# The rotary turn of the second block's queries and key: products on TensorE, or transfers inside SBUF with a signed sine table

## The reference, cut to what matters

```python
half = HEAD_DIM // 2                                  # 32
ang = positions[..., None] * inv_freq                 # inv_freq has 32 values
cos, sin = jnp.cos(ang), jnp.sin(ang)
t1, t2 = tf[..., :half], tf[..., half:]
out = jnp.concatenate([t1 * cos - t2 * sin, t2 * cos + t1 * sin], axis=-1)
...
q = _rope(q.reshape(b, s, N_Q_HEADS, HEAD_DIM), positions)   # 8 heads of 64
k = _rope(k.reshape(b, s, N_KV_HEADS, HEAD_DIM), positions)  # 2 heads of 64
```

## Time and profile before

| what | value |
|---|---|
| device time, median of 3 runs (lowest to highest) | 1407.65 us (1406.44 to 1407.67) |
| span of the profiled execution (first to last instruction) | 1405.4 us, 20877 instructions |
| what the median has beyond that span | 2.25 us |
| busy: PE, DVE, ACT, POOL | 1387.1, 811.0, 478.8, 128.2 us |
| mean granted TensorE clock | 0.999 of full speed |

### The profile page before, as it was taken

How to read it: one execution, slowest core, us unless ns; L and a number is a source line. 1 busy time by engine, 2 the same in 40 slices (tenths; PEclk the granted TensorE clock), 3 DMA queues, 4 the chain that set the end, 5 groups by cost and what they waited for, 6 DMA issues and landing times.

```text
span 1405.4 us, 20877 instructions
## 1 busy us (share of the span) xinstructions
PE 1387.1 (99%) x8982; PEld 1106.9 (79%) x8982; DVE 811.0 (58%) x1142; ACT 478.8 (34%) x723; POOL 128.2 (9%) x134
## 2 busy tenths in 40 slices
PE   7999999999999999999999999999999999999998
PEld 5687887878778888887778888887887877888886
DVE  7375654646558745354575664546635435776654
ACT  6332324234145343234431221223333233444323
POOL 1020302002002011001210000000040012000000
PEclk9999999999999999999999999999999999999999
DMA  5111211111042333322255542332222333211362
GB/s 189 60 46 32 76 32 62 46 46 61 32 166 93 102 126 114 106 75 76 90 180 190 198 166 93 102 97 90 90 90 75 98 97 105 90 61 61 97 172 90
DMA packets 42204, 136.15 MB, mean 97 GB/s; under 512 B 4649, under 2 KB 8361, under 8 KB 42112
## 3 DMA queue, kind: packets, MB, share of 16 engines
q1 hardware_dynamic: 33984, 114.57, 25.3%
q0 software_dynamic: 4080, 14.65, 2.7%
q10 hardware_dynamic: 4048, 5.59, 1.2%
HBM read 130.34 MB, written 2.10 MB: 94 GB/s over the span
## 4 chain that ended last, share of the span: by engine, by line
PE 94%; DVE 3%; DMA 1%; ACT 1%; issue 0%; ACTq 0%; DVEq 0%
PE bank L418 92%; PE bank L421 2%; DVE w_lo L1424 1%; DVE opA_lo L1432 1%; DMA xT<-x 1%; DMA w_raw<-panels 0%; DVE tmp L1432 0%; ACT scores L934 0%; DVE P L1432 0%; ACT w_hi L934 0%; DVE scores L1424 0%; ACT opA_hi L934 0%; DVE sine L1432 0%; DVE cosine L1432 0%; DVE angle L1428 0%
## 5 line engine op out<-in xcount | busy, mean ns | idle before, releaser
L1424 DVE TENSOR_TENSOR w_lo<-w_raw,w_hi 128x1024 fp32r<-128x1024 f32 (+1 forms) x209 | 256.6, 1228 | 358.9 <-ACT w_hi L934 358.6
L418 PE MATMUL bank<-opA_hi,w_hi 128*128 128x512 f32 x1000 | 410.7, 411 | 11.0 <-DVE opA_lo L1432 8.6
L418 PE MATMUL bank<-opA_hi,w_lo 128*128 128x512 f32 x1000 | 395.9, 396 | 0.0
L418 PE MATMUL bank<-opA_lo,w_hi 128*128 128x512 f32 x1000 | 394.7, 396 | 0.0
L934 ACT ACTIVATE w_hi<-w_raw 128x1024 fp32r<-128x1024 f32 (+1 forms) x209 | 220.1, 1053 | 373.1 <-DMA w_raw<-panels 373.0
L418 PEld LDWEIGHTS bank<-opA_hi,w_hi 128*128 128x128 f32 x1000 | 188.2, 188 | 65.1 <-issue 15.9
L418 PEld LDWEIGHTS bank<-opA_hi,w_lo 128*128 128x128 f32 x1000 | 188.3, 188 | 45.4
L418 PEld LDWEIGHTS bank<-opA_lo,w_hi 128*128 128x128 f32 x1000 | 188.3, 189 | 41.8 <-issue 2.2
L418 PE MATMUL bank<-opB_hi,w_hi 128*128 128x512 f32 x448 | 178.5, 398 | 0.3 <-DVE w_lo L1424 0.3
L418 PE MATMUL bank<-opB_lo,w_hi 128*128 128x512 f32 x448 | 177.2, 396 | 0.0
L418 PE MATMUL bank<-opB_hi,w_lo 128*128 128x512 f32 x448 | 177.2, 396 | 0.0
(11 more groups left out here) (316 smaller groups left out, 1601.9 us busy)
## 6 DMA issues: line engine op xcount, KB each, us to landing
w_raw<-panels SPq DMA_DIRECT2D x208, 512.0 KB, 3.4
ada_w<-ada POOLq DMA_DIRECT2D x24, 512.0 KB, 4.5
xT<-x ACTq DMA_DIRECT2D x1, 2048.0 KB, 14.3
x_tokens<-x_blocks SPq DMA_DIRECT2D x16, 128.0 KB, 3.9
out<-x_tokens SPq DMA_DIRECT2D x8, 256.0 KB, 2.0
memT<-mem ACTq DMA_DIRECT2D x1, 1024.0 KB, 5.8
xT<-x ACTq DMA_DIRECT2D x3, 256.0 KB, 7.6
xT<-x SPq DMA_DIRECT2D x3, 256.0 KB, 7.4
```

Source lines behind the costliest of these rows:

```text
L418: return pe.matmul(o, lhsT, rhs, start=start, stop=stop, skip_group_check=True)
L1424: return ve.tensor_tensor(o, a, b, op)
```

## The change

The matrix `rotate` and the five products with it go. In their place ACT issues 20 transfers from SBUF to SBUF, four for each of the five tiles: each moves 32 rows of 2 KB (64 KB), so that `rotated` holds the tile with the halves of every head swapped. They stand in ACT's stream right after the two transfers at `ub`, behind waits for the eviction of the key and of the last query tile. The sign goes into the sine table: `inv_freq` holds the frequencies negated for the rows of first halves, which leaves the cosine as it was. `rotated` has five buffers now, in the space of `opB`. POOL and DVE wait for all 20 transfers at their first `rope` and no longer for TensorE; their places in the streams are the same. The transposes of the values stay behind `zb` panel 0.

```diff
-        "rotate": np.where((j % 64) < 32, -1.0 * (i == j + 32), 1.0 * (i == j - 32)),
...
-    rot = [place(f"rotated{n}", [NP, S], scores_at + n * TB) for n in range(2)]
+    rot = [place(f"rotated{n}", [NP, S], r_opB + (n if n < 4 else 2 * n) * TB) for n in range(5)]
...  TensorE
-        def rotate(n, t):
-            if 2 <= n < 4:
-                pe.wait_ge(rope_sin, n - 1)
-            mm(bank[ROPE_BANKS[n]][:, :], mat("rotate"), P[:, t, :]).then_inc(rot_mm, 1)
-
-        p.multiply()
-        for i in range(FIRST["ub"] - 2, FIRST["ub"]):
-            pe.wait_ge(left[i % 2], left_after(i))
-        rotate(0, K2)
-        rotate(1, Q2)
-        p.leave()
         p.to("zb")
         p.multiply()
         pe.wait_ge(vb_made, 4)
-        for t in range(1, 4):
-            rotate(1 + t, Q2 + t)
+        for i in range(FIRST["ub"] - 2, FIRST["ub"]):
+            pe.wait_ge(left[i % 2], left_after(i))
         for n in range(4):
             ins = turn(bank[V2_BANK][:, n * NP:(n + 1) * NP], P[:, V2, n * NP:(n + 1) * NP])
...  ScalarE, behind the two loads at "ub"
+        for i in range(FIRST["ub"] - 3, FIRST["ub"] - 1):
+            ac.wait_ge(left[i % 2], left_after(i))
+        for n, t in enumerate((K2, Q2, Q2 + 1, Q2 + 2, Q2 + 3)):
+            for a in range(0, NP, HD):
+                b, c = a + HD // 2, a + HD
+                load(halves_here, rot[n][a:b, :], P[b:c, t, :])
+                load(halves_here, rot[n][b:c, :], P[a:b, t, :])
...  GpSimd, in rope()
-            gp.wait_ge(rot_mm, n + 1)
             if n == 0:
+                gp.wait_ge(halves_here, 20 * 16)
                 gp.wait_ge(trig_done, 2)
...  VectorE, in rope()
-            ve.wait_ge(rot_mm, n + 1)
+            ve.wait_ge(halves_here, 20 * 16)
             ve.wait_ge(trig_done, 2)
-            tt(rot[n % 2][:, :], bank[ROPE_BANKS[n]][:, :], sinT[:, :], ALU.mult).then_inc(rope_sin, 1)
+            tt(rot[n][:, :], rot[n][:, :], sinT[:, :], ALU.mult).then_inc(rope_sin, 1)
             ve.wait_ge(rope_sin, n + 1)
             ve.wait_ge(rope_pool, n + 1)
-            tt(dst, dst, rot[n % 2][:, :], ALU.add).then_inc(rope_done, 1)
+            tt(dst, dst, rot[n][:, :], ALU.add).then_inc(rope_done, 1)
...  host
-        "inv_freq": np.tile(freq, 4),
+        "inv_freq": np.concatenate([-freq, freq, -freq, freq]),
```

More of the change, by code:

```diff
@@ L48 @@
 MATS = [("ident", 128), ("mean", 128), ("head_sum", 128), ("cumsum", 128), ("chunk_mask", 128),
-        ("rotate", 128), ("causal", 128), ("eye", 64), ("level1_turned", 64)] + [(f"level{s}", 64) for s in LEVELS[:-1]]
+        ("causal", 128), ("eye", 64), ("level1_turned", 64)] + [(f"level{s}", 64) for s in LEVELS[:-1]]
 MAT = {}
@@ L121 @@
 TOKEN_BANKS = ((4, 5), (6, 7), *((j, 2 + j) for j in (FIRST["out2"] % 2, 1 - FIRST["out2"] % 2)))
-ROPE_BANKS, V2_BANK = (6, 7, 6, 7, 2), 3
+V2_BANK = 3
 F2_LAST = 16 * KT - 2 - 4 * (F2_MAX + F2_SOFTMAX + F2_OUT)
@@ L401, in build @@
         sem("token_spread"), sem("x4_scaled"))
-    angle_step, trig_done, rot_mm, rope_pool, rope_sin, rope_done = (
-        sem("angle_step"), sem("sine"), sem("rotated"), sem("rope_cosine"), sem("rope_sine"), sem("rope_made"))
+    angle_step, trig_done, halves_here, rope_pool, rope_sin, rope_done = (
+        sem("angle_step"), sem("sine"), sem("swapped_halves_here"), sem("rope_cosine"), sem("rope_sine"), sem("rope_made"))
     vb_made = sem("gating_values_made")
```

## The result

The changed kernel takes 1410.2 us (median of 17 runs, 1408.6 to 1411.29), the kernel before 1407.65 us. The ratio is 1.0016 with an interval of 1.0009 to 1.0023: slower by 2.5 us, where I had forecast 3.0 us less. The difference is smaller than the 2.8 us that the prediction took as the limit of what can be told from no change; with 17 executions of each kernel the interval leaves out 1 all the same. The time lies outside the range of 1403.2 to 1408.2.

What follows compares the result with a forecast made beforehand. TensorE, busy 99% of the span, was taken as the bound. Span 1405.4 - 4.28 (products) + 1.28 (stall) = 1402.4 us, plus 2.25 us of median above span, gave 1404.65 us; range 1403.2 to 1408.2.

Steps and rivals of the forecast that it cites:

- What the products are worth: TensorE's unbroken run: removing five rotated products at 0.857 us each gains 4.28 us in all.
- What replaces them and where it hurts: ACT's stream at `ub`: 20 issues delay high part, table load and Gelu; TensorE waits 1.28 us for `ub` panel 2's bank.
- The formula for the stall: TensorE ahead of `ub` panel 2: stall = 20 x (cost of an issue) - 8.3 us, nothing below 0.415 us an issue.
- The cost of an issue: ACT's stream at `ub`: 0.48 us for each of the 20 issues, 9.6 us together; range 0.36 to 0.635.
- the sum: Whole kernel: 1405.4 - 4.28 + 1.28 = 1402.4 us of span, with a stall of 1.28 us at `ub` panel 2.
- The rival with SP's price: ACT's issues at `ub` cost 0.635 us each as on SP: 4.4 us of stall, 1407.8 us, no change; chance 0.22.
- What a standstill costs: TensorE at `ub` panel 2: the stall is taken once, 1.28 us, and then the distance is as before.
- DVE and POOL: `za` and `zb`: low parts have 2 us or more to spare, rotary instructions run alone at 0.69, no cost.
- The transfers' bytes: 1.31 MB beside the panels' 512 KB each from `ub` on: last lands near 1107.5, 39 us of cover, no cost.
- The rule of the Trainium skill: ACT's issues at `ub`: dispatch about 50 ns, so 20 issues an estimated 1 us, hidden in idle time, no stall.
- The 2.25 us above the span: Whole kernel: the median of the runs stands 2.25 us above the traced span; kept, giving 1404.65 us.

Runs made afterwards that it cites:

- the repeated kernel: The changed kernel unaltered, measured again beside the one with 18 dead products added, on the same chip: 1410.6 us, ratio 1.0016 to the kernel before.
- the filled standstill: The changed kernel plus 18 dead TensorE products of 0.233 us right ahead of `ub` panel 2: 1408.07 us, ratio 1.0001 to the kernel before.
- the GpSimd version: The changed kernel with all 20 transfers issued by GpSimd instead of ScalarE: 1403.3 us against 1407.91 for the kernel before, ratio 0.9967.

## Why the prediction was wrong, point by point

- **What the products are worth** (4.28 us): right. Without anything in their place the kernel gained 4.1 us, with the transfers on GpSimd 4.6, both within their intervals of 4.28.
- **What replaces them and where it hurts**: right in mechanism. The release at `ub` panel 2 is by the Gelu, behind the table load, the high part and the issues. The formula for the stall, 20 x (cost of an issue) - 8.3, gives 4.7 us with the measured 0.65 and 4.24 were seen; the masks' issue, which took 1.03 instead of 1.46, is the difference. In the repeated kernel it took 1.42, and 4.75 were seen.
- **The cost of an issue** (0.48 taken): the mis-sized term. I went by engine and shape and set SP's 0.635 aside for its two dimensions. The right likeness was the pair of memories. It measured 0.65 (0.44 from HBM), which made a stall of 4.24 us where the sum has 1.28. The rival with SP's price forecast a stall of 4.4 us and would have been within 0.2 of it.
- **What a standstill costs** (only its own length): the step that failed outright. Every case of the forecast counted a late TensorE as late by that much ("Then the distance is as before"). Standstills of 4.2 to 4.8 us brought 1.6 to 2.8 us at half clock on top. At the 1.28 us of the sum this term might have stayed at nothing: nobody measured a standstill of that length. It is this term that turned "no change", 1407.8 us, into 1410.2 and put the time beyond the range. Without it the forecast's rival would have stood, just inside the range, as the filled standstill shows with 1408.07.
- **DVE and POOL**: DVE's rotary instructions take 0.69 throughout, no gap at `zb` panel 2, as said. The low part beside GpSimd's three cosine products took 3.62 us instead of 1.23, 2.4 more, where I had counted on "2 us or more to spare"; it was 3 us early, so it cost nothing.
- **The transfers' bytes** (nothing): no cost for 64 KB pieces, as the GpSimd version shows, though its panel came 1.8 us later under ScalarE's idle time; with four of 320 KB the panel landed late, which the forecast did not look at.
- **The rule of the Trainium skill** weighed there, that issuing is small relative to the transfer ("DMA: Bandwidth & Descriptors", "Issuing engines are not separate DMA queues"): here the issue took 0.61 us and the transfer landed after 2.6 us, and what counted was the sum of 20 in one engine's stream. The 50 ns stand in a section on transfers issued by GpSimd, and my estimate of 1 us put the making of the descriptors at nothing; it was not a fair reading for ScalarE, and GpSimd's own issue took 0.50 us. The rows were the better guide, and I did not follow them far enough.
- **The 2.25 us above the span**: harmless. Each execution of the experiments takes 1.3 us more than its own span; by the other 1 us the traced execution before was quicker than the median one. With nothing in the products' place the medians came to 1403.3 to 1403.8, where this sum has 1403.4.

## What to carry to other kernels

An issue of a transfer is an instruction of the engine that makes it. Count issues times price at the place where they stand, against the idle time of that engine at that place; give them to an engine that has nothing behind them, spread them, or join them, but with a look at what long transfers push aside. When TensorE is made to wait for 2 us or more, price the wait twice: its length, and the slow products behind it, here 1.6 or 2.8 us. And for an operation that the trace does not show, take the dearer of two likenesses as the forecast if the other one rests on an assumption about why it is dear.

## What the hardware showed that was not expected

- Issued by ScalarE, a transfer with both ends in SBUF costs 0.61 us behind another (0.51 to 0.62 for the first of a run), one from HBM 0.44 to 0.45 (0.35 for the first). On SyncE the transfers inside SBUF of the earlier trace rows have a median of 0.60, a panel from HBM takes 0.33. On ScalarE 32 or 128 rows of 2 KB make no difference. Issued by GpSimd the same transfer from SBUF takes 0.50, less than on ScalarE:

```profile
L925 ACTq DMA_DIRECT2D rotated<-P x20: 514/612/639, 1095.8 to 1108.2; - x20
```

```profile
L1273 POOL DMA_DIRECT2D rotated<-P x20: 496/497/528, 1092.0 to 1101.4; - x20
```

(minimum, median and maximum in ns of one issue, first and last start; the changed kernel, then the GpSimd version).

- The same issue of the window masks took between 0.78 and 1.78 us in twelve executions, at the same place in the stream. What it waits for stays open.
- The clock fell to half by a standstill of 2.04 us, at a price of 1.6 us; one of 1.03 us (due at 402.31, started at 403.34, in the trace before) and those of 0.3 to 0.4 us left it at full. What is lost does not grow with the standstill and differs between executions (2.8 and 1.6 us for the same kernel). Between 1.03 and 2.04 us nothing was measured.
- The clock can dip without a standstill: from 1050 to 1060, around runs of products of a single column, its average lies between 1.00 and 0.77 in twelve traces with the same instructions there.
- VectorE's low part, two inputs in SBUF, takes 1.23 us alone and 3.62 beside three GpSimd products. The 2.4 us more are nearly the 2.53 us for which the two overlap (1158.43 to 1160.96):

```profile
1157.13 3.83 POOL L1277 TENSOR_TENSOR P<-P,cosine 128x512 f32<-128x512 f32 x3
```

```profile
1158.43 3.62 DVE L1419 TENSOR_TENSOR w_lo<-w_raw,w_hi 128x1024 fp32r<-128x1024 f32 x1 [0.78 <-ACT w_hi L922]
1161.98 0.68 DVE L1419 TENSOR_TENSOR P<-bank,tmp 128x512 f32<-128x512 f32 x1
```
